# Turning x for the mixer stages by a product with a diagonal matrix in place of a transpose of a normalised copy

## The reference

```python
def rmsnorm(x, g):
    x32 = x.astype(jnp.float32)
    y = x32 * lax.rsqrt(jnp.mean(x32 * x32, axis=-1, keepdims=True) + EPS)
    return (y * g.astype(jnp.float32)).astype(x.dtype)
...
    for layer in range(DEPTH):
        mod = c_act @ w_ada[layer] + b_ada[layer]
        sh1, sc1, g1, sh2, sc2, g2 = jnp.split(mod[:, None, :], 6, axis=-1)
        h = rmsnorm(x, mix_norm_g[layer]) * (1.0 + sc1) + sh1
        ...
        x = x + g1 * y
        h = rmsnorm(x, ffn_norm_g[layer]) * (1.0 + sc2) + sh2
        x = x + g2 * hierarchical_moe(h, ...)
```

## Time and profile before

| | |
|---|---|
| median of 3 runs | 1248.93 us (1248.77 to 1249.11) |
| the profiled execution | 1248.45 us, its span 1246.7 us |
| granted TensorE clock, mean of the span | 0.875 |
| PE busy / weight loads | 899.5 us (72%) / 441.3 us (35%) |
| DVE busy | 317.6 us (25%) |
| ACT busy | 164.9 us (13%) |
| DMA | 490.07 MB, 393 GB/s in the mean |

### The profile page before, as it was taken

The page is one execution under the profiler, slowest core; times in us unless marked ns, Lnnn a source line. Parts: engine busy times, 40 slices in busy tenths (PEclk is TensorE's granted clock), DMA queues, the critical chain, the costliest instruction groups (busy, mean ns, idle before and its releaser), DMA issues.

```text
span 1246.7 us, 14714 instructions
## 1 busy us (share of the span) xinstructions
PE 899.5 (72%) x6138; PEld 441.3 (35%) x6138; DVE 317.6 (25%) x855; ACT 164.9 (13%) x395; POOL 21.7 (2%) x70
## 2 busy tenths in 40 slices
PE   5999997657574756656799999957475666665647
PEld 5767553122231212121288554522131212121212
DVE  2297463121111111111121154421111111202011
ACT  1113340000000000000133254300000000000000
POOL 1001100000000000000000000000000000000000
PEclk9999999788787878877899999988787978878788
DMA  9999989999999999999994386999999999999996
GB/s 346 369 411 409 390 351 427 427 427 428 428 428 428 428 428 427 429 427 428 407 408 162 135 328 279 357 430 427 428 427 427 428 428 428 428 429 427 428 422 249
DMA packets 62779, 490.07 MB, mean 393 GB/s; under 512 B 7793, under 2 KB 8194, under 8 KB 40194
## 3 DMA queue, kind: packets, MB, share of 16 engines
q1 hardware_dynamic: 59024, 486.59, 93.9%
q10 hardware_dynamic: 3698, 2.66, 0.7%
HBM read 488.19 MB, written 1.05 MB: 392 GB/s over the span
## 4 chain that ended last, share of the span: by engine, by line
DMA 51%; PE 41%; SPq 3%; DVE 3%; issue 1%; ACT 1%; POOL 0%; DVEq 0%
PE psum L1471 41%; DMA weight_ring<-in_moe_w_gate 18%; DMA weight_ring<-in_moe_w_down 18%; DMA weight_ring<-in_moe_w_up 14%; SPq L469 2%; DMA weight_ring<-in_even_w_in 2%; SPq L478 1%; PE psum L1550 0%; DVE h_or_mix_T L1043 0%; DVE phase_region L1430 0%; PE psum L2027 0%; DVE phase_region L1456 0%; DVE phase_region L1013 0%; SPq L461 0%; DVE phase_region L1148 0%
## 5 line engine op out<-in xcount | busy, mean ns | idle before, releaser
L1471 PE MATMUL psum<-weight_ring,h_or_mix_T 128*32 128x512 f32 (+1 forms) x2240 | 382.9, 712 | 237.4 <-DMA weight_ring<-in_moe_w_gate 147.5
L1471 PEld LDWEIGHTS psum<-weight_ring,h_or_mix_T 128*32 128x32 f32 (+1 forms) x2240 | 119.6, 136 | 487.2 <-issue 484.7
L1471 PE MATMUL psum<-weight_ring,ada_partials 128*32 128x512 f32 x1024 | 137.7, 696 | 79.2 <-DMA weight_ring<-in_moe_w_down 74.1
L1471 PE MATMUL psum<-phase_region 128*128 128x128 f32 (+5 forms) x816 | 153.4, 351 | 4.0 <-DVE x_tokens L1274 1.3
L1471 PEld LDWEIGHTS psum<-phase_region 128*128 128x128 f32 (+2 forms) x816 | 97.4, 189 | 73.7 <-issue 53.5
L1471 PE MATMUL psum<-h_or_mix_T,weight_ring 128*128 128x256 f32 (+1 forms) x528 | 114.5, 374 | 3.2 <-DMA weight_ring<-in_even_w_in 1.8
L1471 PEld LDWEIGHTS psum<-h_or_mix_T,weight_ring 128*128 128x128 f32 x528 | 97.5, 190 | 17.2 <-DMA weight_ring<-in_even_w_in 2.0
L1471 PEld LDWEIGHTS psum<-weight_ring,ada_partials 128*32 128x32 f32 x1024 | 39.1, 126 | 165.6 <-issue 158.6
L1333 DVE TENSOR_TENSOR phase_region<-psum,gate_rows 128x512 f32<-128x512 f32 x32 | 22.1, 692 | 227.2 <-PE psum L1471 227.2
L1320 DVE SCALAR_TENSOR_TENSOR phase_region<-phase_region,psum 128x512 f32<-128x512 f32 x16 | 11.0, 688 | 247.3 <-ACT phase_region L865 247.3
L1325 DVE SCALAR_TENSOR_TENSOR ada_partials<-phase_region,psum 128x512 f32<-128x512 f32 x16 | 16.8, 1051 | 211.5 <-PE psum L1471 211.5
(11 more groups left out here) (205 smaller groups left out, 469.9 us busy)
## 6 DMA issues: line engine op xcount, KB each, us to landing
weight_ring<-in_moe_w_up SPq DMA_DIRECT2D x64, 2048.0 KB, 20.3
weight_ring<-in_moe_w_down SPq DMA_DIRECT2D x64, 2048.0 KB, 20.1
weight_ring<-in_moe_w_gate SPq DMA_DIRECT2D x62, 2048.0 KB, 21.0
weight_ring<-in_w_ada SPq DMA_DIRECT2D x10, 3072.0 KB, 19.2
weight_ring<-in_odd_w_in SPq DMA_DIRECT2D x6, 2048.0 KB, 25.2
weight_ring<-in_w_ada SPq DMA_DIRECT2D x10, 1024.0 KB, 21.2
weight_ring<-in_w_ada SPq DMA_DIRECT2D x4, 2048.0 KB, 18.4
weight_ring<-in_even_w_in SPq DMA_DIRECT2D x4, 2048.0 KB, 20.8
```

Source lines behind the costliest of these rows:

```text
L1471: return pe.matmul(out_, lhsT, rhs, start=first, stop=last, **kw)
```

## The change

`normalise` no longer writes a normalised copy of x. It multiplies the 128x128 identity by the block's column of inverse root mean squares into `DIAG`, which lies over the scratch `TMPA`. `turn_xn` takes, in stages 0 and 2, tiles of `X` itself with a stride as the stationary operand and multiplies them with the diagonal by an ordinary product; the result in PSUM is the turned and normalised tile, as before. Stages 1 and 3 keep the transposes.

```diff
+        DIAG = TMPA
...
             def normalise(stage, t):
                 dve.wait_ge(norm_stat, 2 * stage + t + 1)
-                if stage:
-                    src, dst = X[:, t, :].rearrange("p (q k) -> p k q", k=KD), XN[:, t, :, :]
-                else:
-                    src = X[:, t, :].rearrange("p (h q k) -> p h k q", h=2, k=KD // 2)
-                    dst = XN[:, t, :, :].rearrange("p (h k) q -> p h k q", h=2)
-                v.tensor_scalar(dst, src, STAT[:, 2 + t:3 + t], None, ALU.mult).then_inc(xn_ready, 1)
+                v.tensor_scalar(DIAG[:, t, :], IDENT[:, :], STAT[:, 2 + t:3 + t], None, ALU.mult).then_inc(xn_ready, 1)
...
                     pe.wait_ge(xn_ready, 2 * stage + t + 1)
-                    src = XN[:, t]
+                    if stage:
+                        src = X[:, t, :].rearrange("p (q k) -> p k q", k=KD)
+                    else:
+                        src = X[:, t, :].rearrange("p (h q k) -> p h k q", h=2, k=KD // 2)
                 for b, bank in enumerate(turned_banks(stage, t)):
                     for k in range(4):
-                        ins = pe.transpose(PS[:, bank, k * P:(k + 1) * P], src[:, 4 * b + k, :], IDENT[:, :])
+                        into = PS[:, bank, k * P:(k + 1) * P]
+                        if stage % 2:
+                            ins = pe.transpose(into, src[:, 4 * b + k, :], IDENT[:, :])
+                        else:
+                            ins = mm(into, src[:, 4 * b + k, :] if stage else src[:, b, k, :], DIAG[:, t, :], True, True,
+                                     skip_group_check=True)
                     ins.then_inc(xn_turned, 1)
```

## The result

The changed kernel takes 1254.14 us (median of six runs, 1252.92 to 1254.62) against 1248.85 for the kernel before on the same chips; the ratio is 1.0039 with a 95% interval from 1.0028 to 1.0049. That lies above the forecast of 1249.6 and above its range. The profiled execution took 1254.10 us, 5.65 more than the one before.

What follows compares the result with a forecast made beforehand. DMA and TensorE were taken to carry nearly all of the chain. Stage 0's +0.85 us and stage 2's -0.2 summed to +0.65, giving 1249.1 us for a profile and 1249.6 for the median; range 1248.2 to 1251.3.

Steps and rivals of the forecast that it cites:

- the price of a record on PE: Turns of stages 0 and 2: each product record takes 0.213 us at half pace, 0.111 at full pace.
- the rise: Stage 0: PE's pace doubles at 14.75 or 15.75 us, so the turns end at 16.1 or 16.6.
- The rival on the slower side: Stages 0 and 2: strided stationary reads add 54 ns a record, losing 2.0 and 1.1 us; 1252.0 us, chance 0.08.
- The deciding point: Turns: from some 0.04 us extra a record, the strided read's loss passes 0.2% (2.5 us).
- The diagonal: DVE ahead of each turn: the 128x128 instruction that replaces the copy takes 284 ns.
- A product costs twice a transpose: PE turns: a product makes two records, 0.222 us at full pace, against 0.103 for a transpose.
- One for one to the end: Stages 0 and 2: each microsecond lost or won there is carried in full to the kernel's end.
- the starved stretch of the DMA engines: At 180 to 185 us DMA is only 30% busy, waiting for PE; it would move by stage 0's loss.
- The order in stage 2: Stage 2: DVE is free earlier, ACT's last bank isn't waited for, and the projection starts 0.2 us sooner.
- The early-rise rival: Stage 0: ordinary products raise the pace about 0.66 us after starting, at 11.2; total -0.2, 1248.7 us; chance 0.11.
- the 14 to 16 us: Opening: a doubling of PE's pace outside this window would show the prediction wrong.
- The other reading, by which transposes don't count: Opening: the pace doubled 0.66 us after the first ordinary matmul, not 4.2 after the first transpose; held less likely.

Runs made afterwards that it cites:

- first probe: Kernel before plus 88 unread PE operations behind stage 2's turns; products of x took 0.112 us a record packed, 0.231 at stride 8; no total time given.
- experiment 2: Kernel before, with stages 0 and 2 turning the packed normalised copy by ordinary products with the identity instead of transposes; ratio 1.0017.
- experiment 3: Kernel before with the diagonal and the products of x in stage 0 only; ratio 1.0015.
- experiment 7: Changed kernel without the eight products with the identity between the two first half sums; 1252.24 us, ratio to before 1.0027.
- experiments 1, 5, 6 and 8: Kernel before: 1, 5, 6 add unread PE operations behind stage 2's turns (no total given); 8 multiplies GpSimd's packed x copy with the diagonal in stage 2, 1.0009.
- stage 2 alone: Kernel before with the diagonal and the products of x in stage 2 only; ratio 1.0025.

## Why the prediction was wrong

**The step that failed** is the price of a record on PE. I took 0.213 us slow and 0.111 fast; 0.233 and 0.237 were measured. At half pace the line price hides almost wholly (0.233 for 0.213), at full pace it is more than double. In stage 0 this means that the doubling of the pace, worth 0.1 us on each record behind it, was lost; in stage 2 it means 32 x 0.126 = 4.0 us more of PE work. With the measured spacing my own sums give the result: in stage 0 PE begins at 10.79 (the statistic came 0.15 later than in the trace before), 32 x 0.233 leads to 18.25, the half sums start at 18.43, and block 1 follows at 28.2 for 25.42: +2.8. In stage 2 the first bank of block 1 is ready at 627.36 + 24 records of 0.237 + 0.4, at 633.4 as measured, and DVE and PE follow. The order of the work and the way in which a delay is carried on were right; the largest term was mis-sized. In stage 0 the rise was mistaken as well, at 16.5 for 14.75 to 15.75: with the prediction's own prices it would put the end of the turns at 17.1 for 16.1 to 16.6, and the price of the records adds the other 1.2 us to 18.25 (an estimate, as no kernel here has packed products with that rise).

**Why I mis-sized it.** The rival on the slower side named the stride, but priced it from how much longer the load of a strided transpose lasts, 54 ns, and then argued this away by the pace of the strided transposes of stages 1 and 3. The first probe shows that a transpose is no witness: it runs at 0.111 us a record with x at stride 8, the product beside it at 0.231. The extra is some 120 ns at full pace and 20 at half pace, not 54 at both, and with the measured spacings the rival's losses (2.0 and 1.1 us, 1252.0) become 2.8 and 3.1, 1254.8. The deciding point it gave, 0.04 us a record, was passed three times over. A chance of 0.08 rested on one row of a different operation. Why the transpose is spared stays open: no run here shows what differs in its read.

**Right, and confirmed.** The diagonal costs 0.29 us (0.284 forecast). A product costs twice a transpose in records (32 for 16), and 2.0 us for both stages when packed (experiment 2): I had counted 0.65 for packed products with the earlier start by the diagonal, so there is no contradiction, but this part of the change was a loss from the outset and not a trade. One for one to the end: the stretches between the stages differ by 0.06 and 0.04 us, and the starved stretch of the DMA engines moved with stage 0, by the windows of the changed kernel (columns as in rows 4):

```profile
180.00:185.00 5.00, 4.51 (x36) 4.06 (x35) 3.45 (x18) 0.00 (x0) 0.00 (x0) 1.00 0.80 334
183.00:188.00 5.00, 5.00 (x47) 3.10 (x49) 4.05 (x10) 2.46 (x5) 0.00 (x0) 1.00 0.31 131
```

The 30% that stood at 180 to 185 us before stand at 183 to 188. The order in stage 2 was right as well: DVE is free early, ACT's second bank is not waited for. What changed places is who comes last.

**The rise of the pace.** The early-rise rival falls: in experiment 2 ordinary products ran from the first and the pace doubled after 3.0 us, not 0.66. In the changed kernel it rose 5.7 us after the first product, by the same reading 6.4 in experiment 3 and 6.2 in experiment 7. That lies outside the 14 to 16 us which the prediction named as a sign of being wrong, but costs the strided records nothing, since their spacing is the same on either side. With transposes ahead of it the distance was 4.2 us in the run before, 4.4 to 4.7 in the kernels of experiments 1, 5, 6 and 8, whose opening is untouched (the same reckoning, from first half sums of 2.40 to 2.54 us), and 6.0 in the kernel with stage 2 alone. The other reading, by which transposes don't count, isn't borne out in the size that it had in my sum either: packed products alone needed 3.0 us, and behind transposes the pace rose 0.7 to 1.2 us after the first half sum, once 2.4. What sets the instant stays open. The prediction had the granted clock as not on record this early; the windows give it as 1.00 for the whole opening, although the transposes take 422 ns there and 273 later, so all of this goes by durations.

## What to carry to other kernels

Before a tile that other work reads in place becomes an operand of an ordinary product on TensorE, count how many of its elements lie in each 16-byte line of a partition: f32 at stride 2 is nearly free, at strides 4 to 8 each record of 128 columns takes 0.22 to 0.24 us instead of 0.11, on the stationary and the moving side alike. For the stationary side 256 moving columns hide most of it, and at 512 none was seen. A packing copy of a block of x takes DVE 1.15 us and saves 16 records 0.12 each, 1.9 us of PE; transposes can take the strided tile as it is. And price an operation from rows of its own kind: the length of an overlapping record, or the pace of a sibling operation, bounds nothing, so where no row of the kind exists, the range must not be closed by an argument from them.

## What the hardware showed that I had not expected

- The price of lines on either operand of a product: 0.112 us a record at two or more f32 elements a line, 0.174 at stride 3, 0.215 to 0.232 at one; on the moving side runs of 2 within a line 0.112, across a line 0.215.
- Transposes of the same strided tile: 0.111 us a record.
- A strided record takes 0.233 us in stage 0, before the pace rises and after it, and 0.237 in stage 2: the read and not the array sets it, so a faster pace of the engine buys nothing there.
- The instant at which the pace doubles in the opening moved by about 2 us between two kernels with the same opening (15.75 and 17.6 us), and with it the first gather by 1.5 us. It came 3.0 us after the first of packed products, 4.2 to 6.0 after the first of transposes with half sums behind them, 5.7 to 6.4 after the first of strided products.
- A DVE copy of 128x256 took 0.83 us beside copies of GpSimd, 0.29 without.
